# Feed-forward gated product in a hybrid HGRN2/MLA block: transposed by one VectorE instruction per block inside partition quarters, its 32x32 squares carried between quarters by 16 SBUF-to-SBUF transfers

## The reference, cut to what matters

```python
h = rms_norm(x, ffn_norm_w[layer])                       # (256, 2048)
gate, up = jnp.split(h @ w_gate_up[layer], 2, axis=-1)   # (256, 5632) each
x = x + (jax.nn.silu(gate) * up) @ w_down[layer]         # w_down: (5632, 2048)
```

## Time and profile before

| what | value |
|---|---|
| runs, us | 1150.52, 1150.61, 1150.83 (median 1150.61) |
| profiled execution, span | 1148.4 us; its own time is not listed apart, and the median of the runs is 2.2 us above the span |
| granted TensorE clock | 1.000 |
| PE busy | 1137.7 us, 99% |
| DVE, ACT busy | 739.7 us (64%), 575.6 us (50%) |
| DMA | 213.16 MB, queue of SP 59.7% of 16 engines |
| chain that ended last | PE 93%, DVE 4%, ACT 2%, DMA 1%, issue 1% |

### The profile page before, as it was taken

One profiled execution on the slowest core, in us unless ns is written; L12 is line 12 of the kernel. 1 busy time (PEld: TensorE's weight loads), 2 busy tenths in 40 slices (PEclk: granted clock), 3 DMA queues, 4 the chain that ended last, 5 costly groups with the idle time before them and its releaser, 6 DMA issues.

```text
span 1148.4 us, 15834 instructions
## 1 busy us (share of the span) xinstructions
PE 1137.7 (99%) x5382; PEld 958.5 (83%) x5382; DVE 739.7 (64%) x1047; ACT 575.6 (50%) x818; POOL 11.8 (1%) x63
## 2 busy tenths in 40 slices
PE   8999999999999999999999999999999999999999
PEld 7988888887888888888888888888888888888887
DVE  5688787587866575657657657667667565454543
ACT  7567766668654465344344344344344343334342
POOL 3000000000000000000000000000000000000000
PEclk9999999999999999999999999999999999999999
DMA  8666454455645556666666666666666556555654
GB/s 263 199 189 207 140 165 139 150 170 165 204 164 165 165 172 181 198 194 192 189 195 197 186 198 190 194 195 191 194 189 195 190 198 193 192 191 193 198 187 144
DMA packets 113759, 213.16 MB, mean 186 GB/s; under 512 B 7049, under 2 KB 18098, under 8 KB 113458
## 3 DMA queue, kind: packets, MB, share of 16 engines
q1 hardware_dynamic: 112850, 209.30, 59.7%
q0 software_dynamic: 560, 3.15, 0.9%
q10 hardware_dynamic: 304, 0.14, 0.0%
HBM read 210.46 MB, written 2.10 MB: 185 GB/s over the span
## 4 chain that ended last, share of the span: by engine, by line
PE 93%; DVE 4%; ACT 2%; DMA 1%; issue 1%; SPq 0%; DVEq 0%; ACTq 0%
PE main L1295 58%; PE main L1298 29%; PE side L1433 1%; DVE w_lo L847 1%; DMA raw<-in_w_in 1%; PE side L1332 1%; ACT w_hi L580 1%; DVE hbT L1070 0%; PE side L1465 0%; PE side L1367 0%; ACT junk L602 0%; PE side L1410 0%; PE side L1380 0%; PE side L1381 0%; ACT L619 0%
## 5 line engine op out<-in xcount | busy, mean ns | idle before, releaser
L847 DVE TENSOR_TENSOR w_lo<-raw,w_hi 128x1024 fp32r<-128x1024 f32 (+3 forms) x401 | 479.0, 1198 | 370.9 <-ACT w_hi L580 367.2
L580 ACT CAST w_hi<-raw 128x1024 fp32r<-128x1024 f32 (+3 forms) x401 | 411.8, 1030 | 531.6 <-PE main L1295 524.2
L1295 PE MATMUL main<-w_hi,hT_hi 128*128 128x512 f32 (+2 forms) x1088 | 422.6, 389 | 1.7 <-DVE hT_lo L868 1.4
L1298 PE MATMUL main<-w_hi,hT_lo 128*128 128x512 f32 (+2 forms) x1088 | 418.3, 385 | 0.0
L1295 PE MATMUL main<-w_lo,hT_hi 128*128 128x512 f32 (+2 forms) x1088 | 285.6, 384 | 0.0
L1295 PEld LDWEIGHTS main<-w_hi,hT_hi 128*128 128x128 f32 x1088 | 204.8, 188 | 40.2 <-DVE hT_lo L868 1.6
L1298 PEld LDWEIGHTS main<-w_hi,hT_lo 128*128 128x128 f32 x1088 | 205.1, 189 | 37.9
L1295 PEld LDWEIGHTS main<-w_lo,hT_hi 128*128 128x128 f32 x1088 | 203.1, 188 | 38.9
L1298 PE MATMUL main<-w_hi,aT_lo 128*128 128x512 f32 x344 | 133.9, 389 | 0.0
L1295 PE MATMUL main<-w_hi,aT_hi 128*128 128x512 f32 x344 | 133.9, 389 | 0.0
L1295 PE MATMUL main<-w_lo,aT_hi 128*128 128x512 f32 x344 | 92.0, 389 | 0.0
(11 more groups left out here) (208 smaller groups left out, 568.3 us busy)
## 6 DMA issues: line engine op xcount, KB each, us to landing
raw<-in_w_gate_up SPq DMA_DIRECT2D x176, 512.0 KB, 4.4
raw<-in_w_down SPq DMA_DIRECT2D x88, 512.0 KB, 3.6
raw<-in_w_in SPq DMA_DIRECT2D x64, 512.0 KB, 3.9
raw<-in_w_out SPq DMA_DIRECT2D x32, 512.0 KB, 3.7
raw<-in_w_in SPq DMA_DIRECT2D x15, 384.0 KB, 5.2
raw<-in_w_ukv SPq DMA_DIRECT2D x8, 512.0 KB, 3.9
raw<-in_w_uq SPq DMA_DIRECT2D x8, 384.0 KB, 3.3
raw<-in_w_in SPq DMA_DIRECT2D x8, 320.0 KB, 3.3
```

The costliest lines, as they stand in the source:

```text
L580: copy(w_hi[:, slot, 0:n], raw[:, slot, 0:n]).then_inc(s_hi, 1)
L847: tt(w_lo[:, slot, 0:n], raw[:, slot, 0:n], w_hi[:, slot, 0:n].bitcast(F32), ALU.subtract)\
L1295: m = matmul(banks[t][:, 0:cols], hi[:, at[n], tok], rhs, start=(part == "hi" and k == k_first), stop=(part == "lo" and k == last))
L1298: matmul(banks[t][:, 0:cols], lo[:, at[n], tok], rhs, start=False, stop=False)
```

## The change

The 16 transposes of a block become one instruction on all 128 partitions. It transposes each 32x32 square inside its own quarter of the partitions, into a new buffer `squares` (quarter a, square b). SP then carries square row b of quarter a to quarter b, place a, of `hiddenT` by 16 DMAs of 32 partitions by 1 KB (32 KB each). They are issued at step `MOVE_AT = 10` of the loads, between the wait for granule 10's slot and granule 10's load. `hiddenT` is now ordered by quarter, then by token tile, row tile and row, so `split_hidden` on both engines reads it with strides of 32 elements, by token tile instead of by pairs of row tiles, and waits for the 16 transfers (`s_moved`) instead of for the transposes. SP's first FFN block and both halves of the down projection stand outside of loops now.

```diff
--- before.py
+++ after.py
@@ -119,6 +119,10 @@
 
 Q = 32
 SPLIT_AT = 7
+MOVE_AT = 10
+MOVED = 16 * (P // Q) ** 2
+
+
 
 
 def schedule():
@@ -362,7 +366,11 @@
         aT_lo = sb("aT_lo", [P, DOWN_KT, SEQ], F32R)
         gate = sb("gate", [P, NT, NB])
         hidden = sb("hidden", [P, NT, NB])
-        hiddenT = sb("hiddenT", [P, NB // P, SEQ])
+        squares = sb("squares", [P, P // Q, SEQ])
+        hiddenT = sb("hiddenT", [P, P // Q, SEQ])
+
+        def tokens_of(t):
+            return hiddenT[:, :, :].rearrange("p a (t k r) -> p t k a r", t=NT, r=Q)[:, t, :, :, :]
 
         main = [[ctx.enter_context(nc.psum_tensor(f"main{p}{t}", [P, NB], F32)) for t in range(NT)] for p in range(2)]
         side = [ctx.enter_context(nc.psum_tensor(f"side{n}", [P, NB], F32)) for n in range(SIDE)]
@@ -408,6 +416,7 @@
         s_join = sem("s_join")
 
         s_turned = sem("s_turned")
+        s_moved = sem("s_moved")
         s_ahi = sem("s_ahi")
         s_alo = sem("s_alo")
         s_out = sem("s_out")
@@ -471,24 +480,45 @@
                     dst, src = small_loads[g - 7]
                     sp.dma_start(dst, src, allow_slow_non_contiguous=True).then_inc(s_small, 16)
 
-            with sp.Fori(0, NFF) as i:
+            def move_hidden(turned):
+
+                sp.wait_ge(s_turned, turned)
+                for a in range(P // Q):
+                    for b in range(P // Q):
+                        sp.dma_start(hiddenT[Q * b:Q * (b + 1), a, :], squares[Q * a:Q * (a + 1), b, :])\
+                            .then_inc(s_moved, 16)
+
+            def load_gate_up(i, moves):
+
                 for half in range(2):
                     for k in range(KT // 2):
                         j = half * (KT // 2) + k
                         slot = (G0 + j) % RING
                         slot_free(G0 + j + GU * i)
+                        if moves and j == MOVE_AT:
+                            move_hidden(i)
                         src = w_gu[2 * P * k:2 * P * (k + 1), bass.ds(half * D_FF + NB * i, NB)]
                         sp.dma_start(raw[:, slot, :].rearrange("p (k c) -> p k c", k=2),
                                      src.rearrange("(k p) c -> p k c", p=P)).then_inc(s_raw[slot], 16)
 
-            with sp.Fori(0, 2) as i:
+            load_gate_up(0, False)
+            with sp.Fori(1, NFF) as i:
+                load_gate_up(i, True)
+
+            def load_down(i, moves):
+
                 for j in range(2 * DN):
                     slot = (G1 + j) % RING
                     slot_free(G1 + j + 2 * DN * i)
+                    if moves and j == MOVE_AT:
+                        move_hidden(NFF)
                     k = j % DN
                     src = w_dn[2 * P * k:2 * P * (k + 1), bass.ds(NB * (j // DN) + 2 * NB * i, NB)]
                     sp.dma_start(raw[:, slot, :].rearrange("p (k c) -> p k c", k=2),
                                  src.rearrange("(k p) c -> p k c", p=P)).then_inc(s_raw[slot], 16)
+
+            load_down(0, True)
+            load_down(1, False)
 
             for d in range(3):
                 sp.wait_ge(s_taken[(DOWN + d) % 2], taken(DOWN + d))
@@ -790,10 +820,10 @@
 
             def split_hidden(i):
 
-                for u in range(2):
-                    act.wait_ge(s_turned, (P // Q) * (i + 1))
-                    copy(aT_hi[:, bass.ds(4 * i + 2 * u, 2), :],
-                         hiddenT[:, 2 * u:2 * u + 2, :]).then_inc(s_ahi, 1)
+                act.wait_ge(s_moved, MOVED * (i + 1))
+                for t in range(NT):
+                    copy(aT_hi[:, bass.ds(4 * i, 4), t * P:(t + 1) * P].rearrange("p k (a r) -> p k a r", r=Q),
+                         tokens_of(t)).then_inc(s_ahi, 1)
 
             act.dma_start(vec_rows[0:KT, :], attn_norm_w.rearrange("a (k p) -> (a k) p", p=P)).then_inc(s_attn, 16)
             load_x(act, 1)
@@ -1196,26 +1226,21 @@
                     stt(out=hidden[:, t, :], in0=main[PU][t][:, :], scalar=r_ffn[:, t:t + 1], in1=gate[:, t, :],
                         op0=ALU.mult, op1=ALU.mult).then_inc(s_taken[PU], 1)
 
-            def turn_hidden(i, b):
-
-                if b == 0:
-                    dve.wait_ge(s_taken[PU], taken(FF + 1) + NT * i)
-                to = hiddenT[Q * b:Q * (b + 1), :, :]
-                for a in range(P // Q):
-                    tokens = hidden[Q * a:Q * (a + 1), :, :].rearrange("p t (k c) -> p t k c", c=P)
-                    ins = nc.vector.transpose(
-                        to.rearrange("p k (t c) -> p t k c", t=NT)[:, :, :, Q * a:Q * (a + 1)],
-                        tokens[:, :, :, Q * b:Q * (b + 1)])
-                ins.then_inc(s_turned, 1)
+            def turn_hidden(i):
+
+                dve.wait_ge(s_taken[PU], taken(FF + 1) + NT * i)
+                nc.vector.transpose(squares[:, :, :].rearrange("p b (n r) -> p n b r", r=Q),
+                                    hidden[:, :, :].rearrange("p t (k b c) -> p (t k) b c", b=P // Q, c=Q))\
+                    .then_inc(s_turned, 1)
 
             def split_hidden(i):
 
-                dve.wait_ge(s_turned, (P // Q) * (i + 1))
-                for u in range(2):
-                    dve.wait_ge(s_ahi, 2 * i + u + 1)
-                    at = bass.ds(4 * i + 2 * u, 2)
-                    tt(aT_lo[:, at, :], hiddenT[:, 2 * u:2 * u + 2, :],
-                       aT_hi[:, at, :].bitcast(F32), ALU.subtract).then_inc(s_alo, 1)
+                dve.wait_ge(s_moved, MOVED * (i + 1))
+                for t in range(NT):
+                    dve.wait_ge(s_ahi, 2 * i + t + 1)
+                    hi, lo = [x[:, bass.ds(4 * i, 4), t * P:(t + 1) * P].rearrange("p k (a r) -> p k a r", r=Q)
+                              for x in (aT_hi, aT_lo)]
+                    tt(lo, tokens_of(t), hi.bitcast(F32), ALU.subtract).then_inc(s_alo, 1)
 
             def add_down(d):
 
@@ -1258,8 +1283,8 @@
                     convert(n % RING, n + GU * i)
                     if j == 0:
                         multiply_gate(i - 1)
-                    if 2 <= j < 2 + P // Q:
-                        turn_hidden(i - 1, j - 2)
+                    if j == 2:
+                        turn_hidden(i - 1)
                     if j == SPLIT_AT:
                         split_hidden(i - 1)
             for j in range(4 * DN):
@@ -1268,8 +1293,8 @@
                     convert(n % RING, n)
                 if j == 0:
                     multiply_gate(NFF - 1)
-                if 2 <= j < 2 + P // Q:
-                    turn_hidden(NFF - 1, j - 2)
+                if j == 2:
+                    turn_hidden(NFF - 1)
                 if j == SPLIT_AT:
                     split_hidden(NFF - 1)
                 if j and j % DN == 0:
```

## The result

Nine runs of the changed kernel gave 1152.16 to 1154.42 us, median 1153.43; nine of the kernel before gave 1150.52 to 1151.02, median 1150.66. The ratio is 1.0024, 95% interval 1.0014 to 1.0033: 2.8 us slower. The forecast was no change, so the sign is the one of rival 1, and its size is a small part of what that rival threatened (1161 to 1177 us). The profiled execution took 1153.20 us, its span 1151.5; before, the span was 1148.4.

A forecast was written before the change was run, and what follows sets the result against it. PE, full in the FFN, was taken to bound the kernel; DVE's relief and SP's issues lay within slack, so the terms summed to 0 on PE: 1150.6 us predicted. Range 1149.5 to 1152, up to 1161 with a mild stall.

The forecast's parts named there:

- rival 1: In the FFN, granule 10's load comes too late and PE stalls once a block: 1161 to 1177 us, chance 0.14.
- What bounds the kernel: In the FFN PE is full and nobody keeps it waiting; granule 10's load may be 9.4 us late.
- DVE's transpose: On DVE, eleven large transposes at 1.74 us replace 176 small ones: some 58 us less, of which PE gets nothing.
- SP's 16 issues: On SP's queue, 0.47 us per transfer, 7.5 us in all, delays granule 10's load; 1.9 us spare, nothing lost.
- The point from which PE stalls: For the transfers on SP's queue, PE stalls from about 0.59 us from start to start.
- mild case: Late load of granule 10 at 0.65 us per transfer: PE loses 1.0 us a block, 11 us, 1161.
- What is queued behind: Granules 11 and 12 behind the late load are still made before PE wants them, granule 11 with 2.1 us spare.
- The new wait: `split_hidden` on ACT and DVE waits for the last transfer, landed at 578.0; ACT arrives at 581.8, so it is hidden.
- Strides of `split_hidden`: On ACT and DVE, reading runs of 32 elements makes no change; twice as long would cost 1.1 us.
- DMA engines: In the FFN, 512 KB more per block raises their busy share from 0.66 to about 0.70 to 0.75.
- Rival 2: The 16 transfers are served one after the other; PE loses some 18 us a block, 1350 us; chance 0.02.
- Rival 3: A freer DVE makes PE faster in the FFN, at most 58 us, 1093; chance 0.02, shared with any unseen gain.

The follow-up runs named there:

- e1_none: The changed kernel without the 16 transfers, both engines reading `squares` directly: 1150.89 us, ratio 1.0002 to the kernel before.
- e5_hbm: The changed kernel with the 16 transfers reading 32 rows of 1 KB from `w_down` in device memory instead of `squares`: 1150.45 us, ratio 0.9997 to the kernel before.
- e10_at11: The changed kernel with `MOVE_AT` 11 instead of 10: 1153.11 us, ratio 1.0023 to the kernel before.
- e7_late: The changed kernel with `MOVE_AT` 12 instead of 10, two loads later: 1167.08 us, ratio 1.0145 to the kernel before.
- e6_wide: The changed kernel with four transfers of 128 partitions by 1 KB instead of 16 of 32 partitions: 1151.16 us, ratio 1.0004 to the kernel before.
- e3_twenty: The changed kernel with four more transfers of the same size, into a buffer nobody reads: 1199.87 us, ratio 1.0421 to the kernel before.
- e9_at9: The changed kernel with `MOVE_AT` 9 instead of 10: 1167.80 us, ratio 1.0151 to the kernel before.

## Why the prediction was wrong

*What bounds the kernel* was right: PE is full, and 65 us less of DVE are worth nothing (e1_none shows that relief without the transfers).

*DVE's transpose*: 1239 ns where 1.74 us were taken. Between 256 elements in 436 ns and 1024 in 1239 lie 803 ns for 768 elements, 1.05 ns each, over a fixed 0.17 us (an estimate from these two points). It is beside PE's work; all that followed is that DVE was through with granule 6, and SP free to begin, 0.2 us sooner.

***SP's 16 issues* is the step that failed**, by its size. The text took 0.47 us from one start to the next, between 0.37 and 0.52; it is 0.627 (10.04/16). With it the load of granule 10 goes out 10.2 us behind the first transfer, not 7.5, and PE waits 0.2 us and more in ten blocks where nothing was to be lost. The rows for the price were chosen by the size of the transfer, and all of them have their source in device memory. e5_hbm shows that for such a source 0.47 would have been right to 0.02 us; from SBUF to SBUF it is 0.17 us more per issue, and no row of before goes that way (the one with a source in SBUF, writes to device memory). The bound of 0.52 was too narrow for a form that the trace did not contain.

*The point from which PE stalls*, about 0.59 us, was close, and that is what decided. The measured 0.627 is 0.6 us beyond it over 16 transfers. A landing of 3.8 us in place of 4.4 and a start 0.4 us sooner (DVE 0.2 us, and the addresses, which are now computed behind the transfers) gave 1.0 back; 0.2 us for these addresses between the last transfer and the load, and PE's need, which is that of its weight load, 0.3 us ahead of the first matmul's row, took 0.5. So some 0.2 us of waiting was left in most blocks, 0.5 in three, 1.1 in the last and none in one. That these errors nearly cancel is luck: by the prediction's own chain 0.627 gives 0.6 to 0.7 us a block, some 7 us and 1158, and 1153.4 was measured. Rival 1 had this mechanism, place and threshold, at 0.14; its mild case, 1.0 us a block and 1161, overstated it, in part since its price was put at 0.65. The text's own threshold lay 0.07 us above its own upper bound, with a landing time that can be 0.8 us longer. A chance of 0.80 for no stall was too much for that.

*What is queued behind* was right: granule 11 and 12 were never the ones PE waited for. *The new wait* was hidden as said (ACT meets the split behind granule 10), and e10_at11 and e7_late show what happens when this cover goes. *Strides of `split_hidden`*: 616 ns against 617, no change, as taken. *DMA engines*: 0.64 and 0.59 busy against 0.66 and 0.57; the forecast of 0.70 to 0.75 was too high, and nothing hung on it. *Rival 2* is excluded: the transfers land 1.8 us after their issue, issued 0.63 us apart. *Rival 3* is excluded by e1_none.

## What to carry to other kernels

Moving work from a half-idle engine to a DMA queue is no gain in itself, and the queue's own program has to be costed as an engine: so many issues, each with a price that depends on source and destination and hardly on size, and in order behind them the load that feeds the kernel's bound. Compute the slack of exactly that load (from slot free to the bounding engine's need), and when a term of it has no row, treat a threshold near its bound as undecided. If issues must go there, a few ahead of each of several loads, or an idle engine's queue, cost nothing where one block of them does.

## What was not expected of the hardware

A DMA of 32 or of 128 rows of 1 KB from SBUF to SBUF holds SP's queue for 0.59 to 0.60 us, back to back with others (after, e6_wide); one of 32 rows from device memory to SBUF holds it for 0.42 (e5_hbm). In e3_twenty a pause of PE of 2.7 to 2.9 us, in ten blocks, was followed by matmuls at the lower clock (0.61 over the four microseconds shown), 1.5 us of loss a block beyond the pause, while the pauses of 1.2 to 2.2 us in e7_late and e9_at9 were not. One pause of 2.8 us in e7_late was not either; why is open.
